# Prompt attention in a hybrid decoder step: score products of two heads back to back on their row groups, value products alternating between the column groups

## The reference

```python
def masked_softmax(s, mask): ...
# sparse attention: 8 heads of 64, keys of 2 groups; once each for compressed, selected, window keys
p = masked_softmax(einsum('btghd,bsgd->bghts', qg, k) * scale, mask)
o = einsum('bghts,bsgd->btghd', p, v)
# fox: 4 heads of 64
s = einsum('bthd,bshd->bhts', q, k) * scale + cum_q - cum_k      # causal mask, softmax, times v
# stick-breaking: 4 heads of 64
z = einsum('bthd,bshd->bhts', q, k) * scale                       # strict causal mask
w = exp(log_sigmoid(z) + after);  o = einsum('bhts,bshd->bthd', w, v)
```

## Time and profile before

| | |
|---|---|
| time, median of 3 runs | 3377.14 (3375.03 to 3377.66) |
| span of the profiled execution | 3368.1 |
| TensorE busy (matmul rows) | 3184.9, 95% |
| VectorE, ScalarE, GpSimd busy | 606.5, 400.6, 149.5 |
| prompt attention, layer 1 | about 385 to 925 |
| prompt attention, layer 2 | about 2035 to 2575 |

### The profile page before, as it was taken

How to read it: one execution, slowest core, us unless ns; L and a number is a source line. 1 busy time by engine, 2 the same in 40 slices (tenths; PEclk the granted TensorE clock), 3 DMA queues, 4 the chain that set the end, 5 groups by cost and what they waited for, 6 DMA issues and landing times.

```text
span 3368.1 us, 40659 instructions
## 1 busy us (share of the span) xinstructions
PE 3184.9 (95%) x14318; PEld 2384.8 (71%) x14318; DVE 606.5 (18%) x1254; ACT 400.6 (12%) x924; POOL 149.5 (4%) x236
## 2 busy tenths in 40 slices
PE   6999999998799999999999999999989999999997
PEld 5878744454488878888878795444446888888886
DVE  2111244411000110000020214443110111100002
ACT  1010022112211010000011001221122010000000
POOL 0000011111000000000000001111100000000000
PEclk9999999988899999999999999998989999999998
DMA  5342132233322122212413321331432222122120
GB/s 165 123 89 66 51 92 89 73 91 98 101 60 76 67 75 75 75 60 69 135 61 101 85 70 57 96 94 45 128 94 85 75 75 72 54 75 75 52 86 26
DMA packets 304829, 272.80 MB, mean 81 GB/s; under 512 B 59282, under 2 KB 274498, under 8 KB 304370
## 3 DMA queue, kind: packets, MB, share of 16 engines
q1 hardware_dynamic: 287826, 260.55, 25.6%
q10 hardware_dynamic: 16800, 9.61, 1.0%
HBM read 260.48 MB, written 17.97 MB: 83 GB/s over the span
## 4 chain that ended last, share of the span: by engine, by line
PE 90%; DVE 3%; issue 2%; ACT 2%; SPq 1%; POOL 1%; DMA 0%; ACTq 0%; POOLq 0%; DVEq 0%
PE ps L551 18%; PE ps L552 18%; PE ps L1006 9%; PE ps L651 7%; PE ps L522 6%; PE ps L588 5%; PE ps L589 5%; PE ps L698 3%; PE ps L857 3%; PE ps L929 3%; PE ps L737 2%; PE ps L924 1%; PE ps L848 1%; PE ps L765 1%; PE ps L769 1%
## 5 line engine op out<-in xcount | busy, mean ns | idle before, releaser
L551 PE MATMUL ps<-hT,ring 128*128 128x260 f32 x2176 | 657.6, 384 | 10.4 <-DVE hT L1301 10.4
L552 PE MATMUL ps<-hT,ring 128*128 128x260 f32 x2176 | 656.4, 383 | 0.0
L551 PEld LDWEIGHTS ps<-hT,ring 128*128 128x128 f32 x2176 | 414.9, 191 | 75.1 <-DVE hT L1301 11.2
L552 PEld LDWEIGHTS ps<-hT,ring 128*128 128x128 f32 x2176 | 414.9, 191 | 64.3
L1006 PE MATMUL ps<-PT,ring 128*128 128x260 f32 x1408 | 309.1, 383 | 1.7 <-DVE PT L1581 1.7
L1006 PEld LDWEIGHTS ps<-PT,ring 128*128 128x128 f32 x1408 | 267.4, 190 | 43.5 <-issue 2.5
L651 PE MATMUL ps<-arena,ring 128*128 128x127 f32 (+1 forms) x1024 | 238.8, 407 | 0.0
L588 PE MATMUL ps<-hT,ring 128*128 128x260 f32 x704 | 215.4, 388 | 13.2 <-DMA ring<-in_w_in 8.1
L651 PEld LDWEIGHTS ps<-arena,ring 128*128 128x128 f32 x1024 | 209.7, 206 | 24.4
L589 PE MATMUL ps<-hT,ring 128*128 128x260 f32 x704 | 214.2, 386 | 0.0
L551 PE MATMUL ps<-PT,ring 128*128 128x260 f32 x512 | 158.4, 392 | 7.9 <-DVE PT L1572 4.5
(11 more groups left out here) (243 smaller groups left out, 2505.3 us busy)
## 6 DMA issues: line engine op xcount, KB each, us to landing
ring<-in_w_in SPq DMA_DIRECT2D x20, 2048.0 KB, 8.2
units<-in_cache_fox_kv SPq DMA_DIRECT2D x256, 128.0 KB, 2.2
units<-in_cache_sb_kv SPq DMA_DIRECT2D x256, 128.0 KB, 2.2
ring<-in_w_ffn_gate SPq DMA_DIRECT2D x22, 1024.0 KB, 5.4
ring<-in_w_ffn_up SPq DMA_DIRECT2D x22, 1024.0 KB, 7.9
ring<-in_w_ffn_down SPq DMA_DIRECT2D x16, 1408.0 KB, 6.3
units<-in_cache_nsa_cmp_kv SPq DMA_DIRECT2D x128, 128.0 KB, 2.2
units<-in_cache_nsa_sel_kv SPq DMA_DIRECT2D x256, 64.0 KB, 1.8
```

The costliest lines, as they stand in the source:

```text
L551: mm(ps[:, b, 0:H2], w, a[:, 0:H2], start=k == 0, stop=k == n - 1)
L552: last = mm(ps[:, b + 1, 0:H2], w, a[:, H2:T], start=k == 0, stop=k == n - 1)
```

## The change

Three things are done. In `scores` both heads' products now stand first, then (in fox) both forget products, then both masks. In `values` the products of head 0 and head 1 alternate for each key block. In `stick` the four products stand first, then the four masks. For fox, `onehot` and `ncum` are now there on partitions 0 to 3 and 64 to 67, with zeros between, so that each head's forget product uses 64 rows on that head's own partitions; VectorE clears `ncum` once at the start and writes it twice per layer.

```diff
@@ -209,7 +209,7 @@
         l32 = sb("l32", [32, 1])
         bfb = sb("bfb", [P, DEPTH, 4])
         gam = sb("gam", [P, 2 * DEPTH + 1, KD])
-        ncum = sb("ncum", [4, SEQ])
+        ncum = sb("ncum", [P, SEQ])
         ckP = sb("ckP", [P, 2, 32])
         cvP = sb("cvP", [32, P])
         cbias = sb("cbias", [P, 2])
@@ -685,21 +685,22 @@
                 qt = heads(idx)
                 if n >= 1:
                     pe.wait_ge(sems["exp_done"], at(pe, "exp_done", l, n))
+                w = NCP if br == "cmp" else (i + 1) * P
                 for hh in range(2):
                     r = slice(hh * DH, (hh + 1) * DH)
-                    o = ps[:, hh, :]
-                    q = PT[r, qt, i * P:(i + 1) * P]
+                    kt = {"sel": SELK, "win": WINK}.get(br) or FXK + idx - 4
+                    keys = ckP[r, 0, 0:NCP] if br == "cmp" else PT[r, kt, 0:w]
+                    mm(ps[:, hh, 0:w], PT[r, qt, i * P:(i + 1) * P], keys, start=True, stop=True, skip_group_check=True)
+                if br == "fox":
+                    for hh in range(2):
+                        r = slice(hh * DH, (hh + 1) * DH)
+                        h = 2 * (idx - 4) + hh
+                        mm(ps[:, hh, 0:w], C("onehot")[r, h * P:(h + 1) * P], ncum[r, 0:w], start=False, stop=True, skip_group_check=True)
+                for hh in range(2):
                     if br == "cmp":
-                        mm(o[:, 0:NCP], q, ckP[r, 0, 0:NCP], start=True, stop=True, skip_group_check=True)
-                        last = mm(o[:, 0:NCP], identb, mcmpb[:, i * 32:i * 32 + NCP], start=False, stop=True, skip_group_check=True)
-                        continue
-                    kt = {"sel": SELK, "win": WINK}.get(br) or FXK + idx - 4
-                    w = (i + 1) * P
-                    mm(o[:, 0:w], q, PT[r, kt, 0:w], start=True, stop=True, skip_group_check=True)
-                    if br == "fox":
-                        h = 2 * (idx - 4) + hh
-                        mm(o[:, 0:w], C("onehot", 4)[:, h * P:(h + 1) * P], ncum[:, 0:w], start=False, stop=True, skip_group_check=True)
-                    last = mm(o[:, i * P:w], identb, mcausal, start=False, stop=True, skip_group_check=True)
+                        last = mm(ps[:, hh, 0:NCP], identb, mcmpb[:, i * 32:i * 32 + NCP], start=False, stop=True, skip_group_check=True)
+                    else:
+                        last = mm(ps[:, hh, i * P:w], identb, mcausal, start=False, stop=True, skip_group_check=True)
                 last.then_inc(sems["s_ps"], 1)
 
             def turn(l, n, hh):
@@ -727,15 +728,16 @@
                     pe.wait_ge(sems["o_ev"], at(pe, "o_ev", l, idx))
                 for hh in range(2):
                     r = slice(hh * DH, (hh + 1) * DH)
-                    o = ps[r, 3, :]
                     if br == "cmp":
-                        last = mm(o, cvP[0:NCP, r], PTb[0:NCP, hh, 0, :], start=True, stop=True, skip_group_check=True)
-                        continue
+                        last = mm(ps[r, 3, :], cvP[0:NCP, r], PTb[0:NCP, hh, 0, :], start=True, stop=True, skip_group_check=True)
+                if br != "cmp":
                     v = {"sel": 0, "win": 1}.get(br)
                     v = idx if v is None else v
                     for j in range(TT):
-                        last = mm(o[:, j * P:SEQ], vnat[:, v, j, r], PTb[:, hh, j, j * P:SEQ], start=br == "fox" and j == 0,
-                                  stop=True, skip_group_check=True)
+                        for hh in range(2):
+                            r = slice(hh * DH, (hh + 1) * DH)
+                            last = mm(ps[r, 3, j * P:SEQ], vnat[:, v, j, r], PTb[:, hh, j, j * P:SEQ], start=br == "fox" and j == 0,
+                                      stop=True, skip_group_check=True)
                 last.then_inc(sems["pv_done"], 1)
 
             ZO = (0, 512, 1024, 896)
@@ -754,6 +756,7 @@
                 for j in (0, 1, 3, 2):
                     w = SEQ - j * P
                     mm(zp[:, ZO[j]:ZO[j] + w], PT[r, SBK + f, j * P:(j + 1) * P], PT[r, SBQ + f, j * P:SEQ], start=j != 3, stop=True, skip_group_check=True)
+                for j in (0, 1, 3, 2):
                     last = mm(zp[:, ZO[j]:ZO[j] + P], identb, mstrict, start=False, stop=True, skip_group_check=True)
                 last.then_inc(sems["sbz_ps"], 1)
 
@@ -1280,7 +1283,7 @@
             v.tensor_copy(identb, ident)
             last = v.tensor_copy(maskb[:, P:4 * P], hT[:, :, :].rearrange("p a b -> p (a b)")[:, 0:3 * P])
             last.then_inc(sems["const_ok"], 1)
-            for b in (qn[:, :, :], qs[:, :, :, :], qf[:, :, :, :], pc[:, :], pgb[:, :]):
+            for b in (qn[:, :, :], qs[:, :, :, :], qf[:, :, :, :], pc[:, :], pgb[:, :], ncum[:, :]):
                 last = v.memset(b, 0.0)
             last.then_inc(sems["init_z"], 1)
             dve.wait_ge(sems["init_z"], 1)
@@ -1353,7 +1356,8 @@
                         last = v.tensor_copy(qf[r, f, :, :].rearrange("p b c -> p (b c)")[:, c:c + 36 * 7 + 1:36], PT[r, FXQ + f, SEQ:T])
                 last.then_inc(sems["q_ev"], 1)
                 dve.wait_ge(sems["cum_ps"], at(dve, "cum_ps", l, 1))
-                v.tensor_scalar(ncum[:, :], ps[0:4, 4, :], -1.0, None, ALU.mult).then_inc(sems["cum_ev"], 1)
+                v.tensor_scalar(ncum[0:4, :], ps[0:4, 4, :], -1.0, None, ALU.mult)
+                v.tensor_scalar(ncum[DH:DH + 4, :], ps[0:4, 4, :], -1.0, None, ALU.mult).then_inc(sems["cum_ev"], 1)
 
             def compress(l):
                 dve.wait_ge(sems["new_ready"], at(dve, "new_ready", l, 1))
@@ -1645,7 +1649,9 @@
     q = np.arange(P)[:, None]
     put("mine", (np.where(q < 64, q // 8, q % 32 // 4) == np.arange(8)[None, :]).astype(np.float32))
     put("blk", np.tile(np.arange(1, NBLK - 1), (64, 1)).astype(np.float32))
-    put("onehot", np.repeat(np.eye(4), P, axis=1))
+    onehot = np.zeros((P, 4 * P))
+    onehot[0:4] = onehot[DH:DH + 4] = np.repeat(np.eye(4), P, axis=1)
+    put("onehot", onehot)
     tok = np.arange(TT)[None, :, None] * P + np.arange(P)[:, None, None]
     sees = (np.arange(32)[None, None, :] * STRIDE + CBLK - 1 <= tok) & (np.arange(32) < NCP)
     put("cmp01", sees.astype(np.float32))
```

## The result

| | before | after |
|---|---|---|
| time, median of 4 runs on one chip | 3376.41 (3375.03 to 3377.66) | 3241.08 (3234.94 to 3242.72) |
| ratio | | 0.9598, 95% interval 0.9585 to 0.9612 |
| span of the profiled execution | 3368.1 | 3233.0 |
| TensorE busy | 3184.9 | 3025.9 |
| mean granted clock over the span | 0.960 | 0.967 |

The direction and the overlap of the row groups came as said.

The account below looks back on a forecast made before the run. TensorE was taken to bound prompt attention. Savings of 65.8 per layer, 131.6 for both, less 15.8 of waiting and 0.5 added give 115.3; less 6 for the clock, 109: 3377.1 - 109 = 3268, range 3252 to 3314.

Parts of the forecast that it names:

- The bound: Prompt attention: TensorE bounds it, so a microsecond taken from TensorE is one of the kernel, except where it already waits.
- Row groups side by side: Scores: two heads' products on different row groups and banks run at the same time, as column groups do.
- row groups take turns: Scores, rival: the two heads' products do not overlap, only changes of shape are saved; 3312, chance 0.17.
- overlap by one pass: Scores, rival: head 1's first pass runs beside head 0's second, three pass times instead of two; 3286, chance 0.10.
- Scores of sel, win and fox, values, stick: Prompt attention, savings per layer: sel and win scores 26.4, fox scores 14.1, value products 15.6, stick scores 3.6.
- the waiting: Turns behind GpSimd's scaling: shorter scores come back as waiting, 7.9 per layer, 15.8 in both.
- Scores of cmp: 16 cmp items per layer: each saves 0.38, 6.1 in all, with 3.0 taken back where turns wait for GpSimd.
- What it adds: Start of the kernel: one clearing of 0.48, at most 0.5 once; the second writing of ncum costs nothing.
- rows of zeros cost nothing: Fox forget products on 64 rows: the zeros add no time, as a pass takes its columns' time.
- The clock: Attention: more waits lower the granted clock as in the second stretch; 6 taken off the saving.
- at half clock: Lower end of the range, 3252: savings made at half clock, where each is larger.
- The 9 between span and time: Profiled span 3368.1 is about 9 under the median of 3377.1, taken as fixed.

Follow-up runs that it names:

- e8: The changed kernel, but head 1's score product waits by semaphore until head 0's has ended, and in fox each product waits for the one before; 3328.75.
- e7: The changed kernel, with the samples' fox and stick value products alternating and their scores paired on column groups of 32, with four turned-key buffers; 3192.06.
- e4: The changed kernel with the cmp scores put back to product, mask, product, mask; 3241.41, ratio 0.9601.
- e12: The changed kernel with the fox forget products put back to four rows; 3239.69, ratio 0.9598.
- e10: The kernel before with the new scores and values only in units 0 to 9 (items 0 to 39), and fox forget products on 64 rows everywhere; 3291.65.
- e13: The kernel before with only the fox forget products changed, to partitions 0 to 31 instead of 0 to 3, filled up with zeros; 3366.33.
- e11: The kernel before with only the fox forget products changed, to 64 rows on their head's own partitions, 60 of them zeros; 3347.89.

## Why the prediction was right and where it was wrong

**The bound** held. A microsecond taken from TensorE in prompt attention was a microsecond of the kernel, but for the items that wait for GpSimd, and outside attention no stretch moved by more than 1 us.

**Row groups side by side** held. The bound chosen from the column groups' rows was the right one: 1.13 for four passes of 512 keys. The rivals "row groups take turns" (near 2) and "overlap by one pass" (near 1.5) fell by the same row. e8 shows about what the first would have given, 3328.75; the prediction had 3312 for it.

The Trainium skill, "TensorE: Matmul & The Clock Gate", Part 3, "The mechanism", says that matmuls start and end in strict program order. Taken for each pass of a float32 product, as the prediction took it, the trace disagrees: in e7 the second product's first pass starts at 486.16, ahead of the first product's second pass at 486.61, and the measurement decides. Taken for whole products, it agrees: the first product's passes start no later than the second's.

**Scores of sel, win and fox, values, stick** held within a tenth of their sum: 111.1 without the clock, beside 115.3. The first stretch gave 28.0 for the 28.9 that its terms say (19.8 + 6.1 + 9.4, less 6.4 of the waiting, since some 1.5 of the 7.9 falls in fox). In layer 1 this stretch had nearly the same low time before and after, so it needs no price of the clock. The second gave 35.1, of which 12.0 are the clock's (27.3 at 0.44), and the 23.1 left stand for 25.4 (6.6 + 14.1 + 6.2 less 1.5). A unit's values gave 3.86 - 2.31 = 1.55 beside 1.56. The scores of an item with 512 keys gave 2.34 - 1.18 = 1.16 beside 1.15, and a stick head shrinks from 3.42 to 2.53 where 2.5 was said.

**Scores of cmp** had 6.1 less 3.0 a layer in the sum, 6 in all. e4 puts them between nothing (medians) and 4 (spans), so this term may be too large. More turns wait than I had counted on: 22 a layer, where I said some 20, and 14 before, where I had read 13. In layer 1's first stretch the wait for GpSimd grew by 8.0, where the sum took 6.4 of waiting. That accounts for part of the 4 us by which the terms are too large; a larger part lies in the second stretch, and there I haven't found it.

**What it adds** held as far as it can be seen: the clearing of `ncum` takes 0.48, and the stretch ahead of attention is 0.3 shorter than before, not longer. That the rows of zeros cost nothing holds too (0.96 with 64 rows, 1.06 with four, in e12).

**The clock** is the step that failed: "From this I take 6 for the clock." I had read the low clock of the second stretch as a price of TensorE's waits there, and concluded that a first stretch with more waits would slide towards it. But the first stretch, with 20 us of waits instead of 12, kept its 0.97 (17.1 us low before, 16.7 after), and the second, which got more waits too, rose from 0.86 to 0.93. The low time fell by 54.6 us. At 0.44 each this is 24 us gained where I took off 6: a difference of 30, of which the terms' excess of 4 takes back a part, and the rest is the 26 by which the forecast was too slow. Without the clock's part the kernel would be near 3265, so the overlap and its size were foreseen, and the further gain was not. Why the clock rose stays open, as the runs above say. The row for doing better was there, as can be said now: by its mean clock the second stretch lost 22 us to the low level (0.14 of 158) while TensorE waited for only 13, so a shorter stretch could lose less of it as well as more. A term with both signs open belonged into the range on both sides; mine reached only to savings "at half clock", 3252. The 9 between span and time that I took as fixed was misread too (it is 1.9), but as the forecast is a difference from the median time, it moved nothing.

## What to carry to other kernels

Where two products use different row groups and different banks, or different column groups and so different partitions of a bank, put them next to each other with nothing of another shape in between. In float32 the second was then nearly free here (1.13 for four passes of 512 against 1.12 for two), and the masks of full height go behind both. Count the gain by the periods of the profile, and take off the items whose next step waits for another engine anyway. A stretch with a low granted clock is a term of its own with both signs: price it from the same rows at either level, and set the spans of two kernels against each other only after that, or gains of parts won't add up. Look at the clocks of several executions before a low time is explained.

## What the runs showed of the hardware that I had not expected

- The granted clock of a stretch is not fixed by its instructions. The same matmul rows took 151.9 and 142.1 us in the two layers of one execution (e10, 636 of them), and 162.4 and 149.5 in another (e13, 635), with 41.0 and 17.1, 58.0 and 30.7 us at 1.2 GHz. What decides between them stays open; the number of rows in use (4, 32, 64, 128) doesn't order it, and the order of the first stretch doesn't decide it.
- A microsecond at the low level costs 0.41 to 0.47 in this stretch, a little less than the half that the two levels would give, and near the 0.45 of the scores' own rows (1.22 and 2.22 a head). Ahead of attention 10 us more of it cost under 1 us (after and e11).
- Two neighbouring groups of 32 columns overlap as fully as two of 64: 0.98 for four passes of 512 (e7).
